# Merge and router as one chunked program, and a split of the first expert pair's picked rows

## The reference, cut to what matters

```
ya = (rms_norm(o_a) * silu(za)) @ w_out_a          # branch a, 256 x 1024
yb = (rms_norm(o_b) * silu(rb)) @ w_out_b          # branch b
y  = sigmoid(gates_a) * ya + sigmoid(gates_b) * yb
x  = x + g1 * (y @ w_out)
h  = rms_norm(x) * (1 + scale) + shift
logits = h @ w_router + b_router                   # 32 experts
top_logit, top_idx = top_k(logits, 4);  p = softmax(top_logit)
# expert e, on the tokens that picked it:
gu  = h @ w_gu[e] + b_gu[e];  glu, lin = split and clip
out += p * (((lin + 1) * glu * sigmoid(1.702 * glu)) @ w_down[e] + b_down[e])
```

## Time and profile before

| | |
|---|---|
| three runs, us | 2097.64, 2099.54, 2106.0 |
| the profiled execution, us | 2105.05 |
| its span, first to last instruction, us | 2103.3 |
| mean granted TensorE clock | 0.975 |
| PE / DVE / ACT busy | 91% / 29% / 21% |
| merge stage in the span, about | 568.7 to 740.3 us |
| expert stage, about | 741.2 to 1668 us |

### The profile page before, as it was taken

How to read it: one execution, slowest core, us unless ns; L and a number is a source line. 1 busy time by engine, 2 the same in 40 slices (tenths; PEclk the granted TensorE clock), 3 DMA queues, 4 the chain that set the end, 5 groups by cost and what they waited for, 6 DMA issues and landing times. The chain is left out here.

```text
span 2103.3 us, 24697 instructions
## 1 busy us (share of the span) xinstructions
PE 1919.1 (91%) x9335; PEld 1041.3 (50%) x9336; DVE 615.6 (29%) x1346; ACT 434.7 (21%) x869; POOL 68.9 (3%) x102
## 2 busy tenths in 40 slices
PE   6999997999989889999999888899999889999997
PEld 3336455887878443333333333233333245767775
DVE  1476565246620221110111111101111122432223
ACT  3222641327231111111111111001111022521011
POOL 1000400100000000000000000000000000000000
PEclk9999999899999889999999999999999999999999
DMA  9444348215373669999999999999999872114442
GB/s 360 160 167 146 139 112 200 71 49 180 117 255 140 280 264 420 421 422 422 422 422 422 422 422 422 422 422 422 422 422 422 351 276 85 68 50 152 158 156 103
DMA packets 124901, 567.15 MB, mean 270 GB/s; under 512 B 36064, under 2 KB 45024, under 8 KB 69152
## 3 DMA queue, kind: packets, MB, share of 16 engines
q1 hardware_dynamic: 122528, 560.70, 67.9%
q10 hardware_dynamic: 2304, 5.51, 0.8%
HBM read 555.02 MB, written 11.14 MB: 269 GB/s over the span
## 5 line engine op out<-in xcount | busy, mean ns | idle before, releaser
L2057 PE MATMUL expert_gb<-expert_ring,hT 128*64 128x512 f32 x768 | 203.2, 608 | 40.8 <-DMA expert_ring<-in_w_gu 39.4
L1951 DVE TENSOR_SCALAR hT<-expert_gb 128x512 f32<-128x512 f32 x32 | 22.1, 692 | 704.0 <-PE expert_lb L2057 704.0
L2057 PE MATMUL expert_lb<-expert_ring,hT 128*64 128x512 f32 x768 | 197.9, 594 | 0.0
L2105 PE MATMUL expert_yb<-expert_ring,hT 128*64 128x512 f32 x384 | 167.4, 592 | 0.0
L2105 PE MATMUL expert_yb<-expert_ring,h2T 128*64 128x512 f32 x384 | 167.4, 592 | 0.0
L469 PE MATMUL mix_in_pj<-hT,mix_in_pj_ring 128*128 128x512 f32 (+1 forms) x384 | 144.7, 536 | 1.3 <-DVE hT L589 1.3
L2463 PE MATMUL attend_bank<-hT,expert_ring 128*128 128x256 f32 x640 | 141.4, 379 | 0.0
L2463 PEld LDWEIGHTS attend_bank<-hT,expert_ring 128*128 128x128 f32 x640 | 121.6, 190 | 25.1 <-issue 9.6
L2057 PEld LDWEIGHTS expert_gb<-expert_ring,hT 128*64 128x64 f32 x768 | 46.9, 137 | 166.7 <-DMA expert_ring<-in_w_gu 115.9
L1997 ACT ACTIVATE hT<-hT 128x512 f32<-128x512 f32 x32 | 20.1, 630 | 526.0 <-DVE hT L1951 526.0
L141 PE MATMUL delta_scan_fill_bank<-hT,fill_w 128*128 128x512 f32 (+1 forms) x288 | 104.3, 522 | 8.7 <-DMA fill_w<-in_w_fill 5.9
(11 more groups left out here) (484 smaller groups left out, 2632.6 us busy)
## 6 DMA issues: line engine op xcount, KB each, us to landing
expert_ring<-in_w_gu SPq DMA_DIRECT2D x192, 1024.0 KB, 26.8
expert_ring<-in_w_down_units SPq DMA_DIRECT2D x96, 1024.0 KB, 27.1
late<-in_w_gu SPq DMA_DIRECT2D x32, 1024.0 KB, 25.9
mix_in_wm<-in_w_mod_units SPq DMA_DIRECT2D x11, 2048.0 KB, 9.6
expert_ring<-in_w_up_units SPq DMA_DIRECT2D x22, 1024.0 KB, 6.2
fill_w<-in_w_fill SPq DMA_DIRECT2D x40, 512.0 KB, 3.9
fill_w<-in_w_gu SPq DMA_DIRECT2D x16, 1024.0 KB, 26.8
ob<-in_w_gu SPq DMA_DIRECT2D x16, 1024.0 KB, 26.5
```

The lines of the kernel that those rows point to most:

```text
L1951: v.tensor_scalar(glu, gb[j][:], LIMIT, None, ALU.min).then_inc(s_glu, 1)
L2057: m = pe.matmul(b[halves[h], :], xT[:, k, x], unit[z][:, c0 + 512 * h:c0 + 512 * h + 512], start=False, stop=(k == KT - 1))
L2105: m = pe.matmul(yb[h][halves[j], :], hidT[j][:, c, hh * SLOTS:(hh + 1) * SLOTS], unit[z][:, a * F + 512 * h:a * F + 512 * h + 512], start= ...
```

## The change

Six edits, with the rest of both stages as it was.

1. ACT forms all logarithms, then both exponentials. It empties fill F0+2's bank before the Silu; the Silu is cut in two halves, one per branch, with F0+3's bank emptied between them. The second half waits for its own transfer (`s_pz`), the first no longer does.
2. The product of branch b with its gate and the sum `y` are done per PSUM bank, each as PE finishes it (`s_pb`). The first mixed product waits for the parts of `y` one by one.
3. PE's order at the end: mixed (0,0), (0,1), (1,0), transposes of half 0, mixed (1,1), logits of half 0, transposes of half 1, logits of half 1. ACT and DVE follow the same order.
4. The mean's scale and the epsilon go into ACT's square root; DVE takes the reciprocal after it. Two small DVE instructions become one, per half.
5. The first pair's picked rows are copied out by ACT (four pieces) and DVE (four pieces) side by side.
6. SP's wait before units 0 to 3 counts the four parts of `y`.

```diff
@@ ACT, merge
-                    act.wait_ge(s_ln, n + 1)
-                    act.activation(r[:], r[:], ACT.Exp, scale=-0.5).then_inc(s_rt, 1)
-                act.wait_ge(s_in, 48)
-                act.activation(pz[:, 0:16, :], pz[:, 0:16, :], ACT.Silu).then_inc(s_sil, 1)
-                for f in range(F0 + 2, F1):
+                for n, r in enumerate((ra, rb)):
+                    act.wait_ge(s_ln, n + 1)
+                    act.activation(r[:], r[:], ACT.Exp, scale=-0.5).then_inc(s_rt, 1)
+                keep(F0 + 2)
+                act.wait_ge(s_in, 32)
+                act.activation(pz[:, 0:HA, :], pz[:, 0:HA, :], ACT.Silu).then_inc(s_sil, 1)
+                keep(F0 + 3)
+                act.wait_ge(s_pz, 16)
+                act.activation(pz[:, HA:2 * HA, :], pz[:, HA:2 * HA, :], ACT.Silu).then_inc(s_sil, 1)
+                for f in range(F0 + 4, F1):
                     keep(f)
...
-                    act.activation(rstd[:, t:t + 1], ss[:, t:t + 1], ACT.Sqrt).then_inc(s_rs, 1)
+                    act.activation(rstd[:, t:t + 1], ss[:, t:t + 1], ACT.Sqrt, scale=1.0 / D, bias=C.eps[:]).then_inc(s_rs, 1)
@@ PE, merge
+                def mixed(t, h):
+                    for k in range(KT):
+                        if (t, h) == (0, 0) and k % 2 == 0:
+                            pe.wait_ge(s_y, k // 2 + 1)
...
+                mixed(0, 0)
+                mixed(0, 1)
+                mixed(1, 0)
+                turn(0)
+                mixed(1, 1)
+                logits(0)
+                turn(1)
+                logits(1)
@@ DVE, merge
-                v.wait_ge(s_pa, 2)
                 for b in range(4):
-                    m = v.tensor_tensor(sq[:, 2 * b:2 * b + 2, :], bank[4 + b][:], pz[:, 24 + 2 * b:26 + 2 * b, :], ALU.mult)
-                link(m)
-                v.tensor_tensor(y[:], y[:], sq[:], ALU.add).then_inc(s_y, 1)
+                    if b < 3:
+                        v.wait_ge(s_pb, b + 1)
+                    else:
+                        v.wait_ge(s_pa, 2)
+                    c = slice(2 * b, 2 * b + 2)
+                    link(v.tensor_tensor(sq[:, c, :], bank[4 + b][:], pz[:, 24 + 2 * b:26 + 2 * b, :], ALU.mult))
+                    v.tensor_tensor(y[:, c, :], y[:, c, :], sq[:, c, :], ALU.add).then_inc(s_y, 1)
@@ DVE, experts, first pair only
+                    v.wait_ge(s_gx, first + 1)
+                    for k in range(KT // 2, KT):
+                        m = v.tensor_scalar(xT[:, k, :], xb[k // 4][:, k % 4, :], S.a2[:, k:k + 1], S.b2[:, k:k + 1],
+                                            ALU.mult, ALU.add)
+                    m.then_inc(s_xv, 1)
@@ ACT and PE, experts
-                    take(first)
+                    take(first, KT // 2)
...
+                    pe.wait_ge(s_xv, p + 1)
                     ups(first, 0)
```

More of the change, by code:

```diff
@@ L1545, in merge_route_stage @@
         bank = [s.ps(f"bank{b}", [P, 2, L]) for b in range(8)]
-        (s_in, s_pz, s_wo, s_x, s_sq, s_ss, s_v, s_rt, s_sil, s_ya, s_pa, s_t, s_y, s_z, s_xs, s_n, s_rs, s_tr, s_h, s_xt, s_xta, s_ln, s_sqb) = (
+        (s_in, s_pz, s_wo, s_x, s_sq, s_ss, s_v, s_rt, s_sil, s_ya, s_pa, s_t, s_y, s_z, s_xs, s_rs, s_tr, s_h, s_xt, s_xta, s_ln, s_sqb, s_pb) = (
             s.sem(n) for n in ("in", "branch_gates_in", "wo_in", "x_in", "squared", "sums", "chain", "rooted", "silu", "gated",
-                               "branch", "mixed", "y_done", "out_done", "x_squares", "norm", "rstd_done", "turned", "h_done",
-                               "x_copied", "x_copied_high", "logs_done", "linear_squared"))
+                               "branch", "mixed", "y_done", "out_done", "x_squares", "rstd_done", "turned", "h_done",
+                               "x_copied", "x_copied_high", "logs_done", "linear_squared",
+                               "branch_banks"))
         s_rw, s_tab, s_wa, s_rb, s_br, s_l, s_e, s_p, s_r, s_m = (s.sem(n) for n in (
@@ L1570, in _ @@
                 S.fill.load(sp, F0 + 4)
-                sp.dma_start(pz[:, HA:2 * HA + NPARKED], A.fill_latent[HB + HA:].rearrange("c p n -> p c n")).then_inc(s_in, 16)
+                sp.dma_start(pz[:, HA:2 * HA + NPARKED], A.fill_latent[HB + HA:].rearrange("c p n -> p c n")).then_inc(s_pz, 16)
                 S.fill.load(sp, F0 + 5)
@@ L1637, in _ @@
                 for t in range(2):
-                    act.wait_ge(s_z, t + 1)
+                    act.wait_ge(s_z, 2 * t + 2)
                     act.activation(junk, S.x[:, t, :], ACT.Square, accum_out=ss[:, t:t + 1]).then_inc(s_xs, 1)
-                    act.wait_ge(s_n, 2 * t + 2)
-                    act.activation(rstd[:, t:t + 1], ss[:, t:t + 1], ACT.Sqrt).then_inc(s_rs, 1)
-                for t in range(2):
+                    act.wait_ge(s_xs, t + 1)
+                    act.activation(rstd[:, t:t + 1], ss[:, t:t + 1], ACT.Sqrt, scale=1.0 / D, bias=C.eps[:]).then_inc(s_rs, 1)
                     act.wait_ge(s_tr, t + 1)
@@ L1689, in _, with turn @@
                                           src[:, k, :], start=(k == 0), stop=(k == KT - 1))
+                        if n == 1 and o in (1, 3, 5):
+                            m.then_inc(s_pb, 1)
                     m.then_inc(s_pa, 1)
                 pe.wait_ge(s_wo, 16)
[L1692 to L1699, removed]
+                def mixed(t, h):
+                    for k in range(KT):
+                        if (t, h) == (0, 0) and k % 2 == 0:
+                            pe.wait_ge(s_y, k // 2 + 1)
+                        m = pe.matmul(flat(2 * t + h), y[:, k, t * P:(t + 1) * P],
+                                      w[0][:, k, 512 * h:512 * h + 512], start=(k == 0), stop=(k == KT - 1))
+                    m.then_inc(s_t, 1)
+                def turn(t):
                     pe.wait_ge(s_h, 1 + t)
@@ L1704, in _, with logits @@
                     m.then_inc(s_tr, 1)
-                for t in range(2):
+                def logits(t):
                     pe.wait_ge(s_xt, t + 1)
@@ new lines, in _, with update @@
+                    link(v.tensor_tensor(sq[:, c, :], bank[4 + b][:], pz[:, 24 + 2 * b:26 + 2 * b, :], ALU.mult))
+                    v.tensor_tensor(y[:, c, :], y[:, c, :], sq[:, c, :], ALU.add).then_inc(s_y, 1)
+                v.wait_ge(s_x, 16)
+                def update(t, h):
+                    c = slice(512 * h, 512 * h + 512)
+                    v.wait_ge(s_t, 2 * t + h + 1)
+                    link(v.tensor_tensor(S.xn[:, t, c], bank[2 * t + h][:].rearrange("p a n -> p (a n)"),
+                                         S.g1[:, c], ALU.mult))
+                    v.tensor_tensor(S.x[:, t, c], S.x[:, t, c], S.xn[:, t, c], ALU.add).then_inc(s_z, 1)
@@ L1769, in normed, with turned @@
                 def normed(t):
                     v.wait_ge(s_rs, t + 1)
+                    link(v.reciprocal(rstd[:, t:t + 1], rstd[:, t:t + 1]))
                     v.tensor_scalar(S.xn[:, t, :], S.x[:, t, :], rstd[:, t:t + 1], None, ALU.mult).then_inc(s_h, 1)
[L1773 to L1779, removed]
+                def turned(t):
@@ L1782, in _ @@
                                   .rearrange("p (k n) -> p k n", k=4)).then_inc(s_xt, 1)
+                update(0, 0)
+                update(0, 1)
+                normed(0)
+                update(1, 0)
+                turned(0)
+                update(1, 1)
+                normed(1)
+                turned(1)
                 route = Chain(v, s_r)
@@ L1848, in expert_stage @@
         (s_used, s_sel, s_gx, s_xT, s_selw, s_pt, s_put, s_glu, s_lin, s_sig, s_hid, s_tr, s_trc,
[L1849 removed]
+         s_yc, s_sc, s_ac, s_bs, s_bd, s_mid, s_shift, s_xv) = (s.sem(n) for n in (
              "unit_used", "picks", "gathered", "x_ready", "weights", "put_turned", "put_ready",
              "glu_done", "lin_done", "sig_done", "hid_done", "hid_turned", "hid_copied", "y_copied",
[L1852 removed]
+             "spread", "added", "up_bias_pick", "down_bias_pick", "hid_formed", "shifted", "x_upper_half"))
         def up_done(it, j):
@@ L1986, in _, with take @@
             def _(act):
-                def take(n):
+                def take(n, blocks=KT):
                     act.wait_ge(s_gx, n + 1)
-                    for k in range(KT):
+                    for k in range(blocks):
                         m = act.activation(xT[:, k, :], xb[k // 4][:, k % 4, :], ACT.Identity,
```

24 lines of the change are left out of this document (6 added, 18 removed).

## The result

The changed kernel takes 2083.22 us (median of 5 runs, 2082.57 to 2085.97) against 2099.54 (5 runs, 2096.27 to 2106.0): ratio 0.9914, 95% interval 0.9895 to 0.9933 (the quotient of the two medians is 0.9922, inside the interval). The forecast was 2080, the range 2073 to 2088. The profiled execution took 2083.09 us with a span of 2081.3 at a mean granted clock of 0.980.

The account below looks back on a forecast made before the run. Full DMA from the first reload bounds the stage; PE's path before it, where DMA stands still, sets the end. 8.5 + 5.6 + 3.2 + 1.4 + 2.1 - 1.7 = 19.1 us off 2099.54 gives 2080, range 2073 to 2088.

Parts of the forecast that it names:

- front, with its clock: Merge's fills before branch a: branch a starts 8.5 us earlier, less 1.7 for a clock fall before F0+5.
- `y` by banks and the moved transposes: Start of mixed products: wait and half clock go, 6.7 us; half 0's transposes ahead of the last mixed product cost 1.1.
- after the last mixed product: Transposes and logits up to DVE's read: 12.5 us become 9.3, a gain of 3.2 (2.6 to 4.8).
- split, PE's wait: Copies before the first up products: ACT's four take 1.50 instead of about 2.95 us, gain 1.4, at least 0.2.
- clock at the up products: Bias products and first unit: shorter idle time keeps the clock up, gain 2.1 us, at least 0.
- rival 2: Clock low at the up products as before, low longer in the front (2.4 us): gain 16.3, 2083 us; chance 0.11.
- Rivals 3 and 4: 3: the stream swallows the gain, 2099.5 us, chance 0.05; 4: clock stays low through the first pairs, slower, chance 0.03.

Follow-up runs that it names:

- the split alone: Only edit 5 (first pair's picked rows copied by ACT and DVE side by side) made on the kernel before: 2099.95 us, ratio 0.9988.
- the front alone: Only edit 1 (ACT's new order, Silu in two halves) made on the kernel before: 2097.08 us, ratio 0.9977.
- the kernel with the load first: Changed kernel with F0+5's weight load put ahead of the 1.5 MB of gates in SP's list: 2080.2 us, ratio 0.9896 to the kernel before.
- the order alone: Only edits 3 and 4 (PE's order at the end, epsilon in the square root) made on the kernel before: 2104.78 us, ratio 0.9999.
- `y` alone: Only edits 2 and 6 (`y` by banks, SP's wait for its four parts) made on the kernel before: 2094.74 us, ratio 0.9962.
- the filled gap: Changed kernel with the split undone and eleven products without use between gather and up products: 2087.55 us, ratio 0.993 to the kernel before.

## Why the prediction was right, step by step

All from the first fill on, profile against profile. The steps meet at the starts of branch a and branch b, DVE's reads of the last mixed product and of the logits, the starts of the copies and of the first bias product, and the first reload:

| step | forecast, us | measured, us |
|---|---|---|
| front, with its clock (8.5 - 1.7) | 6.8 | 6.95 |
| branch a to branch b | 0 | -0.04 |
| `y` by banks and the moved transposes (6.7 - 1.1) | 5.6 | 5.83 |
| after the last mixed product | 3.2 | 2.08 |
| routing and gather | 0 | -0.27 |
| split, PE's wait | 1.4 | 1.35 |
| clock at the up products | 2.1 | 2.15 |
| sum, first fill to first reload (187.14 to 169.09) | 19.1 | 18.05 |

**The time.** The forecast of 2080 us was 3 too low: the median fell by 16.3 us and not 19.1. The times alone can't part the forecast from rival 2, whose 2083 is the measured median: the interval of the ratio stands for 14 to 22 us. The profiles do. Their span fell by 22.0 us, since the profiled execution of before lay 5.5 above its median, and 18.05 of that lie on the path of the table.

**The bound.** The claim that everything up to the first used unit moves the end one for one holds: from the first reload to the end of the span it is 1347.25 us before, 1347.5 after, and 1344.1 (the split alone) to 1348.6 (the front alone) over the twelve profiles, while the reload itself moved by 27.2, from 187.14 to as little as 159.94. Rivals 3 and 4 fall.

**Front.** What is late next was named rightly: `fill_w`, 2.22 us where 2.8 was forecast. That the load's place in the queue holds F0+5 is shown by the kernel with the load first. The clock fell in this run at the price taken (5.41 against 3.72, so 1.69), and in three more of the five profiles in which PE idles there; the front alone kept it behind a wait of 2.04 us, so the term could also have come to nothing.

**`y` by banks.** The four sums took 0.69 us each, as read from the rows; the last product and sum took 1.4 us together, and PE waited for none.

**Tail: the mis-sized term.** 9.3 us were taken for what lies between the last mixed product and the logits (ends 7.7 to 9.9); DVE's read comes after 10.48, before after 12.56 (722.20 to this row of the kernel before):

```profile
734.76 0.23 DVE L1789 TENSOR_TENSOR merge_lg<-merge_bank,merge_br 128x64 f32<-128x64 f32 x1 [6.08 <-PE merge_bank L1709]
```

The chain to the transposes is 3.97 (forecast 3.95) and the hand-over 0.78 (0.8), but the transposes took 1.97 and the logits 3.62. The ends came from rows of before in which the clock fell midway (1.69) or in which 32 products ran in one piece (half of 6.88). With the order changed, PE idles 2.30 us ahead of both, and in this run the clock was down before either began. In the order alone and in the kernel with the load first the same transposes took 1.09 and the whole tail 9.60 us; in the other five profiles of the new order without a filled tail they took 1.97 and the tail 10.5. So 0.9 of the 1.1 us missing hangs on when the clock falls.

The 2.08 us themselves are in part luck. The old tail took 12.56 us in the execution of before that the forecast was made from, and 12.44 with `y` alone; in the kernels with the front alone and the split alone, which have the same old tail, it took 9.75 and 9.73, less than the new one. There the mixed products had taken 30.8 and 30.7 us instead of 29.1. From branch b to the logits, both steps together, the changed kernel saves 7.9 us against the profile of before, and 6.8 and 6.7 against those two: which of the two steps gets the gain depends on the clock, the sum much less.

**Split.** DVE's four took 1.36 us, within the 1.3 to 1.4 read from widths, and ACT's 1.50. That the clock then stays up was read from the 1.73 us gap before F0; the filled gap shows idle time as the cause, and 2.15 us as its price.

**Rival 2.** A clock change had no fixed moment from one run to the next: the logits of the old order took 6.88 us in the kernel before, 3.79 and 3.77 in two kernels that had left that part as it was. The Trainium skill (TensorE: Matmul & The Clock Gate, "Part 1: The HAM clock gate") says that the moment varies from run to run for the same kernel; these traces agree. At rival 2's two places it went otherwise than that rival has it: at the up products the clock stayed up, and the front's loss was 1.69 us and not 2.4.

**The rest of the span's 22.0 us.** 4.2 lie ahead of the merge, in code that is the same in both. Over the twelve profiles the merge's first fill starts between 564.70 (the profile after; the next is 567.08) and 570.33 us, whichever edits the kernel holds, so the spans of a single pair of profiles can be off by that much. The ratio is taken over several runs.

## What to carry to other kernels

Look for the stretch in which DMA stands still before a stage that it bounds: what lies on PE's path in that stretch is worth its full length, and little else is. When a wait is removed, ask which transfer is next, and whether its place in the queue, not its size, makes it late. An idle gap of PE of 2 to 3 us often had a second price here, at the lower clock: 2.15 us behind the gap of 2.99 before the up products, 1.69 behind the one of 2.22 before F0+5. Shorten it, or fill it. And where the clock can fall anywhere in a stretch, one profile doesn't price a part of it: look at the same code in several.

## What the runs showed that was not expected

- Work without a result paid. Filling the tail's gaps with products that nobody reads put the first reload 3.9 us earlier than in the profile with the load first (ratios 0.9873 and 0.9896).
- A 512 KB load landed 6.2 us after issue behind 1.5 MB on the same queue and 3.8 us ahead of it; two lines swapped brought branch a forward by 4.4 us.
- Once down, the clock stayed at 0.50 from 709.0 to 728.5 us with PE busy 13.21 of 19.50 us. And nearly equal waits before the same fill ended at either level: F0+5 took 3.72 us after 2.04 us of idle time with the front alone, 5.40 after 2.02 with the up products' gap filled.
